# Two-block kernel, expert slots: the third weight matrix is requested by ScalarE on its own DMA queue instead of by SyncE

## The reference, cut to what matters

```python
hid = jax.nn.silu(jnp.einsum('td,edf->tef', t, w1)) * jnp.einsum('td,edf->tef', t, w3)
hid = hid * combine.astype(hid.dtype)[:, :, None]
y = jnp.einsum('tef,efd->td', hid, w2)
```

## Time and profile before

| | |
|---|---|
| median of three runs | 3004.94 us |
| the profiled execution, its own time | 3012.22 us |
| its span, first to last instruction | 3010.5 us |
| mean granted TensorE clock | 0.917 of full speed |
| PE busy | 2630.8 us (87%) |
| DVE, POOL, ACT busy | 1857.9, 1393.5, 939.4 us |
| SP's queue q1 | 329.29 MB, 33.5% of 16 DMA engines over the whole span |
| POOL's queue q0; ACT's queue q10 | 21.59 MB; 25.71 MB |
| first layer's slots | from 383 to 647 us |
| second layer's slots | from 1203 to 1470 us |

### The profile page before, as it was taken

The page is one execution under the profiler, slowest core; times in us unless marked ns, Lnnn a source line. Parts: engine busy times, 40 slices in busy tenths (PEclk is TensorE's granted clock), DMA queues, the critical chain, the costliest instruction groups (busy, mean ns, idle before and its releaser), DMA issues.

```text
span 3010.5 us, 36825 instructions
## 1 busy us (share of the span) xinstructions
PE 2630.8 (87%) x12788; PEld 2043.3 (68%) x12788; DVE 1857.9 (62%) x2116; ACT 939.4 (31%) x1333; POOL 1393.5 (46%) x838
## 2 busy tenths in 40 slices
PE   4878979968999997899689899999984559999998
PEld 3655667746777775677468357888863458788887
DVE  6768755657677665556548467554258983666424
ACT  2022256633444421566321223221012221322101
POOL 4610323325444442333346015666666735666664
PEclk7977889989999997899889689999996879999999
DMA  8736178852232220788522003333240002333322
GB/s 295 269 115 211 71 253 302 290 201 85 91 98 91 91 77 28 267 295 289 196 68 84 14 15 98 95 93 96 92 119 8 1 1 70 95 93 93 99 95 77
DMA packets 315309, 377.76 MB, mean 125 GB/s; under 512 B 49818, under 2 KB 257454, under 8 KB 315094
## 3 DMA queue, kind: packets, MB, share of 16 engines
q1 hardware_dynamic: 259696, 329.29, 33.5%
q10 hardware_dynamic: 31782, 25.71, 2.8%
q0 software_dynamic: 23744, 21.59, 2.2%
HBM read 395.26 MB, written 50.94 MB: 148 GB/s over the span
## 4 chain that ended last, share of the span: by engine, by line
PE 66%; DVE 16%; DMA 8%; issue 6%; ACT 3%; SPq 0%; ACTq 0%; POOL 0%; DVEq 0%; POOLq 0%
PE PAIR L486 16%; PE PAIR L488 16%; PE PAIR L487 16%; PE PAIR L1652 3%; DMA W2RAW<-in_moe_w 2%; PE BANK L2057 2%; DMA ADA_A<-in_ada_w 2%; DMA XG<-htok_scratch,GATHER_I 2%; PE BANK L1264 2%; PE BANK L486 1%; PE BANK L487 1%; PE BANK L488 1%; DVE ADA_SUM L589 1%; ACT WH L1695 1%; DVE ADA_SUM L591 1%
## 5 line engine op out<-in xcount | busy, mean ns | idle before, releaser
L486 PE MATMUL PAIR<-HH,WH 128*128 128x512 f32 x1792 | 711.1, 397 | 40.0 <-POOL HL L1062 23.4
L773 POOL TENSOR_TENSOR WL<-RAW,WH 128x2048 fp32r<-128x2048 f32 x146 | 701.4, 4804 | 12.2
L487 PE MATMUL PAIR<-HL,WH 128*128 128x512 f32 x1792 | 701.9, 392 | 0.0
L488 PE MATMUL PAIR<-HH,WL 128*128 128x512 f32 x1792 | 701.8, 392 | 0.0
L770 POOL TENSOR_TENSOR TURN<-ONES 128x1 f32<-128x1 f32 x146 | 37.7, 258 | 1035.3 <-PE PAIR L488 960.0
L486 PEld LDWEIGHTS PAIR<-HH,WH 128*128 128x128 f32 x1792 | 339.3, 189 | 122.4 <-issue 38.4
L487 PEld LDWEIGHTS PAIR<-HL,WH 128*128 128x128 f32 x1792 | 339.5, 189 | 71.5 <-issue 2.4
L488 PEld LDWEIGHTS PAIR<-HH,WL 128*128 128x128 f32 x1792 | 339.0, 189 | 71.9
L771 POOL TENSOR_SCALAR WH<-RAW 128x2048 fp32r<-128x2048 f32 x146 | 283.8, 1944 | 0.0
L1750 DVE TENSOR_TENSOR WL<-RAW,WH 128x2048 fp32r<-128x2048 f32 x80 | 186.4, 2331 | 77.1 <-ACT WH L1695 77.1
L1816 POOL DMA_INDIRECT y_scratch<-OG,SCATTER_I x80 | 82.0, 1025 | 241.4 <-ACT OG L1708 226.2
(11 more groups left out here) (480 smaller groups left out, 4826.2 us busy)
## 6 DMA issues: line engine op xcount, KB each, us to landing
RAW<-in_moe_w SPq DMA_DIRECT2D x160, 512.0 KB, 4.7
RAW<-in_ffn_w_up SPq DMA_DIRECT2D x88, 512.0 KB, 4.9
W2RAW<-in_moe_w SPq DMA_DIRECT2D x80, 512.0 KB, 6.7
ADA_B<-in_ada_w SPq DMA_DIRECT2D x30, 1024.0 KB, 5.3
RAW<-in_ssm_w_in SPq DMA_DIRECT2D x48, 512.0 KB, 4.5
ADA_A<-in_ada_w SPq DMA_DIRECT2D x18, 1024.0 KB, 6.9
RAW<-in_ffn_w_down SPq DMA_DIRECT2D x32, 512.0 KB, 4.3
RAW<-in_ev_w_in SPq DMA_DIRECT2D x20, 512.0 KB, 4.7
```

The lines of the kernel that those rows point to most:

```text
L486: nc.tensor.matmul(o, wh, xh, start=start, stop=False)
L487: nc.tensor.matmul(o, wh, xl, start=False, stop=False)
L488: return nc.tensor.matmul(o, wl, xh, start=False, stop=stop)
L773: pool.tensor_tensor(WL[:, s], RAW[:, s], WH[:, s].bitcast(F32), ALU.subtract).then_inc(split_ready, 1)
```

## The change

ScalarE gets a new function `third`: it reads the expert's number of a slot from `SLOT_I` into one of its registers and issues the DMA of the third matrix into `W2RAW` on ScalarE's queue. It is called twice at the start of a layer, behind a wait for `experts` (slots 0 and 1), and in each step behind the copy `OG` of slot s-1, for slot s+1. ScalarE has by then waited for `down` of slot s-1, which is what frees the buffer. SyncE loses `down` with its register load, its wait and its DMA; its loop runs 19 times instead of 18 and asks for gate and up alone. Bytes, buffers, matmuls and copies are the same.

```diff
         def first():
+            act.wait(w["experts"])
+            third(None, 0)
+            third(None, 1)
             weights(None, 0)
             rows(None, 0)
...
+        def third(e, s):
+            expert = act.e.value_load(SLOT_I[0:1, at(turns(e, 2), s)], min_val=0, max_val=EXPERTS - 1)
+            w2 = t["moe_w2"][layer][bass.ds(expert, 1)].rearrange("e d f -> (e d) f")
+            act.e.dma_start(W2RAW[:, s % 2, :], w2).then_inc(w2_landed[s % 2], 16)
...
             if stage(e, s, 1):
                 output(e, s - 1)
+                if stage(e, s, -1):
+                    third(e, s + 1)
...
-        def down(i, s):
-            w2, = weights_of(i, s, "moe_w2")
-
-            if layer or s >= 2:
-                sp.wait_ge(w["down"], i + (SLOTS * layer + s - 1))
-            sp.dma_start(W2RAW[:, s % 2, :], w2).then_inc(w2_landed[s % 2], 16)
-
         up(0, 0)
         up(0, 1)
-        for s in range(2):
-            up(0, s + 2)
-            down(0, s)
-        with sp.Fori(0, SLOTS // 2 - 2) as n:
+        with sp.Fori(0, SLOTS // 2 - 1) as n:
             i = n * 2
             for s in (2, 3):
-                up(i, s + 2)
-                down(i, s)
-        down(0, SLOTS - 2)
-        down(0, SLOTS - 1)
+                up(i, s)
```

## The result

The changed kernel takes 3027.39 us (median of 4 runs, 3019.26 to 3034.65), the kernel before 3003.74 us in the same comparison. The forecast was 3015 us, with slower as the likeliest sign. The profiled execution of the changed kernel is the fastest of its four (3019.26 us, span 3017.5 us), so its slots may show less of the loss than the medians do. A second set of runs gave 3028.38 against 3002.30 us, 1.0082 [1.0065, 1.0099].

What follows compares the result with a forecast made beforehand. It took a two-slot ring of PE, ACT and DVE (11.64 us), ACT without slack, as the pace where no DMA is late. 11.6 - 6 + 2 + 3 = +10.6, rounded to +10, on 3004.9 gave 3015 us; range 2993 to 3042.

Steps and rivals of the forecast that it cites:

- SP's queue: SyncE's loss of 80 register loads, waits and DMAs was to win nothing, 0, since its idle time covers them.
- ACT's issue: ScalarE's register load and issue behind OG were to delay GH, +0.29 us per slot, counted for half of 80: +11.6.
- The third matrix's landing: Asked for earlier, the third matrix was to end almost all 11.6 us of PE's waits for it; counted as -6.
- gate and up's landing: Sharing the DMA engines with the third matrix, gate and up were to land later in the slots: +2.
- Of the 11.6 I count half: Only half of PE's 11.6 us of waits for W2RAW was to become saved time, as gate and up come late next.
- a quarter of 0.6 / 2 over the 30 or so heavy slots: In DMA-heavy slots (440 to 560 us), gate and up's 5.5 + 1.77 = 7.3 us exceeds 6.7 by 0.6: +2.
- The upper bound that was given, +12: The most that later landings of gate and up were to cost in the medians: 0.6 / 2 x 40.
- The start of a layer: Two third matrices requested beside the first gather were to delay it by 1.5 us per layer: +3 (0 to 7).
- Faster: Rival, chance 0.20: PE's waits for the third matrix vanish and ScalarE's requests fit beside OG; -11.6 to -18 us.
- Nothing: Rival, chance 0.25: bytes set the landings, waiting only moves from W2RAW to RAW, ScalarE's work is covered; -4 to +5.
- Slower by much: Rival, chance 0.17: ScalarE's register load and issue run only after the copy OG, +0.8 us per slot; some +40, 3045 us.
- The prediction's sum by that rule, +17: If a second issuing queue saves only sequencer time, the -6 for the third matrix becomes 0 and the total +17.

Runs made afterwards that it cites:

- f_read_early: Changed kernel with ScalarE's register load moved ahead of the copy OG, only the DMA's issue left behind it: 3017.41 us, 1.0045 of the kernel before.
- e_sp_first: Kernel before with SyncE asking for the third matrix ahead of gate and up on its one queue, ScalarE issuing nothing: 3014.96 us, 1.0045.
- f_sp_read_early: Kernel before with SyncE's request for the third matrix 0.7 us sooner, still behind gate and up: 3007.13 us, 1.0008.
- g_act_read2: Kernel before with two register loads on ScalarE behind the copy OG, no DMA added: 3012.16 us, 1.0037.
- g_both: Kernel before with SyncE asking for the third matrix ahead of gate and up, and two register loads on ScalarE behind OG: 3015.85 us, 1.0051.

## Why the prediction was right or wrong, point by point

The forecast was slower by 10 us with a range from 2993 to 3042 us; measured are 3027 us, +24. The sign and the first mechanism were right; the two terms for the landings were mis-sized, and their sum had the wrong sign.

*SP's queue, 0:* right as far as seen. SP's idle time before the change covers what it lost, and it issues gate and up 0.17 us behind WL in both kernels.

*ACT's issue, +11.6:* right, in size and in its steps. GH was forecast at 1.25 and 1.5 us behind OG and came at 1.24 and 1.45 to 1.62. The load of 0.28 us does run beside the copy. In the stretch from 560 on a slot takes 6.17 us instead of 5.93, +0.24 where +0.29 was forecast. Half of 80 slots at +0.29 was a choice, and that the total fits is partly luck: the heavy stretch slowed by as much (6.33 to 6.59), though not by this part alone. Two loads of about the same length, alone, cost 11 us (1.0037). f_read_early, which takes this part out of the changed kernel, lies 0.0037 below it, 11 us; by the medians, each against its own runs of the kernel before, it is 26.1 against 12.5, 13.6 us.

*The third matrix's landing, -6, and gate and up's landing, +2:* this is the step that failed. Together they were to give -4; asking for the third matrix first cost +13 us in f_read_early, and as much in e_sp_first, with SyncE's lateness in it. "Of the 11.6 I count half" took the waits for W2RAW as half lost time. f_sp_read_early removes 4.9 us of them and wins nothing, and without any such load the whole is 6.6 us. The larger part of the error was the factor in "a quarter of 0.6 / 2 over the 30 or so heavy slots": the deficit was set against 5.5 us, the median over both DMAs of a pair. WH needs the second too, and its median was 7.1 us in the heavy stretch, already beyond the 6.7 us that it "may take", so there was no room in half of the ten pairs whose landings the trace has there. It rose to 7.5 there, and from 5.3 to 6.0 in the light stretch, which had been counted as never late; the waits in the slots rose from 8 to 24. The upper bound that was given, +12 "in the medians", was near the measured 13.

*The start of a layer, +3:* the traces show 1.7 us against the kernel before (26.4 and 26.0 us, where it was 25.2 and 25.5), 1.2 of it from the two early requests, and the runs can't tell it from nothing.

*The sum:* 11.6 - 6 + 2 + 3 = 10.6 against 11 + 13.5 = 24.5 for the two parts by the ratios of g_act_read2 and f_read_early, and 24 to 26 for the change. That the parts measured alone add up to it is partly luck: put together in g_both they give only 14 to 15, and 9 us stay open.

*The rivals.* "Faster", by 11.6 to 18 us, is excluded by the result and by the ceiling of 6.6 us (10.2 at most). "Nothing" had its mechanism right, the waiting moves from W2RAW to RAW, but the price was wrong: the exchange isn't even. "Slower by much" named a register load that waits for the copy to end. ScalarE issues the third matrix 0.75 us behind OG's start, with the load done, so that is excluded; GH stays well under 2 us in the medians. Its last sentence, gate and up late everywhere at +12 to +20, came near what happened.

*The rule of the Trainium skill:* the page DMA: Bandwidth & Descriptors, section Issuing engines are not separate DMA queues, says that requests of different engines end on the same 16 DMA engines and that several issuers save only sequencer time. The runs fit it as far as they go: 1.0045 with the early request on SyncE's queue and 1.0045 on ScalarE's, 1.0000 on ScalarE's when it is made late. Whether the 9 us that g_both leaves open have to do with the queue, no run shows. The sequencer time was saved on SyncE, which stood idle 110.6 us of 212, and spent on ScalarE, which had none to give. The prediction's sum by that rule, +17, came nearer, but it holds the same mis-sized +2.

## What to carry to other kernels

A wait that shows in a profile is only worth what the load behind it doesn't need: ask first what the time would be without that transfer at all (here 6.6 us less), before moving requests. The order of requests acted as a priority here, from SyncE's queue and from ScalarE's: keep first what the longest chain needs first. When a wait needs several landings, set its slack against the last of them, not against the median of all. And when an experiment turns an order in one engine's program, look at whether that engine then comes late with what follows, as SyncE did in e_sp_first. If an engine must issue a DMA, put the request under a long instruction, as under WH here (1.93 us), not between two copies that follow each other.

## What the runs showed that had not been expected

Work of ScalarE's sequencer, register loads and the issue of a DMA, runs beside its own copy and is free up to the 0.92 us at which the next copy could start: 0.6 us of it cost nothing (0.9994), 1.1 us cost 11 us. A tiny DMA is not cheaper to issue: 64 bytes out of one row took ScalarE's sequencer 470 ns, 512 KB over 128 partitions 349 ns in the changed kernel and 326 to 457 in the kernel before. And asking for 512 KB per slot some 2.5 us earlier (f_read_early) cost 13 us over 80 slots, while taking it away altogether gave 6.6.
